# Moving the first head norm group between the gaps of the RWKV chunk steps, and HGRN output products with whole value operands

## The chip, the cores and the metric

The kernel runs as one program on one core of a Trainium2 chip. The metric is the time of the device for the whole program, in microseconds (us), the median over runs. TensorE (PE in the profile) does the matmuls, VectorE (DVE) and ScalarE (ACT) the elementwise work and the sums along a row, GpSimd (POOL) a few gathers, SyncE (SP) issues nearly all transfers. The engines run their own instruction lists in order and wait for each other by semaphores.

## The reference, cut to what matters

The program is one streaming step of a two-layer trunk over 256 prompt frames and 64 sample frames (320 in all), model width 1024.

```
layer 0: x = LN(a*x + [RWKV-7 heads | GLA heads] @ w_out);  x = LN(a*x + SwiGLU(x))
layer 1: x = LN(a*x + HGRN2(x) @ w_out);                    x = LN(a*x + top-2-of-8 experts(x))

RWKV-7, a head of 64:  S_t = S_{t-1} (diag(w_t) - kk_t^T (a_t * kk_t)) + v_t^T k_t ;  o_t = S_t r_t
  then per head and frame:  o = (o - mean(o)) * rsqrt(var(o) + eps) * gn_w + gn_b     (the head norm)
GLA / HGRN2:           S_t = diag(exp(log_a_t)) S_{t-1} + k_t^T v_t ;  o_t = q_t S_t
  GLA: 4 heads, keys 64, values 128.   HGRN2: 8 heads, keys 128, values 128.
```

Both recurrences are worked out in chunks of 64 frames: five chunks, numbers 0 to 3 of the prompt and number 4 of the sample. A chunk's output has two parts, one from the state carried into it and one from inside it. All of it is in 32-bit floats; the dense layers split each operand into a high and a low part of the shorter format `fp32r` and take three products.

## The kernel before

Each engine has one hand-written list of instructions. The dense weights come through a ring of four tiles; ScalarE makes the high half (L2441, `wd_hi`), VectorE the low half (L1468, `wd_lo`), and TensorE takes the three products (L596 to L598, or L609 to L613 where the inputs are only just ready). The experts' weights go the same way at the end (L2916, L2184, L1371 to L1397).

**RWKV chunk steps.** `STEPS = [[0, 4], [1], [2], [3]]`: four steps, the first with two chunks. For each step:
- TensorE multiplies the carried state into the step's first product (L712, `turned_pairs`) and VectorE copies it out (L1765, `w1_done`);
- TensorE takes the next product, ScalarE copies it (L2659, `u_done`), TensorE finishes the state's update (L696, `each(dh, ...)`) and then the step's output, which ScalarE copies to `Osb` (L2666, `o_done`);
- VectorE adds and scales the state `H` (L1784, L1785, `h_done`), for which the next step waits.

The head norm works on `Osb` in two groups: places 0 to 2 (the first two steps, 768 columns, `NEARLY = 3`) and places 3 and 4 (512 columns). For each group VectorE sums (L1738, `norm_totals`), scales the sum and subtracts it (L1746, L1747, `norm_centred`), ScalarE squares (L2645), VectorE sums the squares (L1752, `norm_squares`), ScalarE takes Ln and Exp (L2651, L2652, `norm_std`) and VectorE scales (L1758, `norm_scaled`, `gn_done`). TensorE then turns the rows back (`rows_back`, L991): the first group's after `gn_done` 1, the second's after `gn_done` 2. Around them it does the gla updates (L696 again, in a bank that `h_done` 4 frees) and the gla outputs (L805); VectorE makes the four gla states (L1805) in between the instructions of the second group's norm. ScalarE copies the gla outputs (L2588) and rounds the first input of the next dense layer (L2597), and VectorE makes its low part (L1817).

**HGRN.** The projections of the HGRN layer are taken two output blocks of 128 columns at a time, in two halves of the inputs, and between these halves and behind them stand pieces of the attention: rows turned (L1150, L1155), scores of a level (L1133), state updates (L1179, `hgrn_updates`), the carried part of an output (`hgrn_carried(c)`, L1167, once for each of the chunks 1 to 4), and at the end the parts from inside the chunks (`hgrn_inside(h)`, L1201, for the two halves of the heads). VectorE renews the state of a chunk (L2070) after the carried product of the same chunk has read the old one (`hgrn_o_full`). ScalarE copies the carried products out, VectorE adds the inside parts to them (L2087).

The TensorE array of 128 by 128 can be used in parts. In `hgrn_carried` the weights are 128 rows (keys) by 64 columns (half of the values), and the two halves go to the two halves of the output's rows. In `hgrn_inside` the weights are 64 rows (frames) by 64 columns; chunks of even number lie in the lower rows, those of odd number in the upper ones, so four quadrants are used in turn.

Of the kernel before, what the change touches and what calls it, by code (L numbers as in the profile page):

```python
# [19 lines left out]
C = 64  # L20
NCH = T // C
N_PROMPT_CH = T_PROMPT // C
# [19 lines left out]
HH, HD = 8, 128  # L42
# [33 lines left out]
def mixed_trunk(nc, ins, outs):  # L76
    ctx = ExitStack()
    with ctx:
# [206 lines left out]
        he = tok(h_.take(HH * T), HH)  # L285
# [10 lines left out]
        def place_of(c, hh):  # L296

            par, m_ = (c % 2, 4 * (c // 2) + hh) if c < N_PROMPT_CH else (hh // 2, 8 + hh % 2)
            return slice(64 * par, 64 * par + 64), m_
# [148 lines left out]
        def S(name):  # L448
            name = shared.get(name, (name, 0))[0]
            if name not in names:  # L450
                names[name] = sem(name)
            return names[name]

        def at_count(name, value=1):

            return S(name), shared.get(name, (name, 0))[1] + value
# [52 lines left out]
        def chunk(c):  # L509
            return slice(c * C, (c + 1) * C)  # L510
# [42 lines left out]
        def _(pe):  # L553
# [605 lines left out]
            def hgrn_carried(c):  # L1159

                pe.wait_ge(*(at_count("hgrn_s", c) if c < N_PROMPT_CH else at_count("hgrn_state_in", 16)))
                pe.wait_ge(*at_count("hgrn_qk", len(OPERANDS)))
                b = take(("hgrn_carried", c), "hgrn_o", c)
                for f in range(HH):
                    for half in range(2):
                        values = slice(64 * half, 64 * half + 64)
                        mm = pe.matmul(b[values, f * C:(f + 1) * C], hs[:, 0 if c < N_PROMPT_CH else 1, f, values], he[:, f, chunk(c)],  # L1167
                                       start=f == 0, stop=f == HH - 1, skip_group_check=True)
                mm.then_inc(S("hgrn_o_full"), 1)

            def hgrn_updates(first, second):
# [15 lines left out]
            def hgrn_inside(h):  # L1187

                pe.wait_ge(*at_count("hgrn_sc", 2 * (2 * LEVELS + h) + 2))
                for last in range(2):  # L1190
                    two = [take(("hgrn_inside", h, 2 * last + par), "hgrn_sum", 4 * h + 2 * last + par + 1) for par in range(2)]
                    which = [[(2 * par + i, N_PROMPT_CH) for i in range(2)] if last else
                             [(hh, par + 2 * j) for hh in range(4) for j in range(2)] for par in range(2)]
                    n = len(which[0])
                    for i in range(n):
                        for turn_ in range(2):
                            for par in range(2):
                                rows, m_ = place_of(which[par][i][1], which[par][i][0])
                                half = turn_ ^ par
                                values = slice(64 * half, 64 * half + 64)  # L1200
                                mm = pe.matmul(two[par][values, i * C:(i + 1) * C], hv_rows[rows, h, m_, values],  # L1201
                                               h_sc[rows, h, m_, :], start=i == 0, stop=i == n - 1, skip_group_check=True)
                                if turn_ and i == n - 1:
                                    mm.then_inc(S("hgrn_o_full"), 1)

            def hgrn_sums(h):

# [247 lines left out]
        def _(dve):  # L1455
# [199 lines left out]
            def chain_operands(a):  # L1655
                n_, F = a["name"], a["F"]
                dve.wait_ge(*at_count(n_ + "_e", LEVELS + 2))
                dve.tensor_tensor(a["KD"], a["KD"], a["k"], ALU.mult).then_inc(S(n_ + "_qk"), 1)
                dve.wait_ge(*at_count(n_ + "_e", LEVELS + 1))
                dve.tensor_tensor(a["Z"], a["E"], a["q"], ALU.mult)  # L1660
                dve.tensor_copy(ends[:, 0:F, :], a["E"].rearrange("p f (c t) -> p f c t", c=NCH)[:, :, :, C - 1])\
                   .then_inc(S(n_ + "_qk"), 1)
# [98 lines left out]
            for i, step in enumerate(STEPS):  # L1761
                n = len(step)
                place = PLACE[step[0]]
                dve.wait_ge(*at_count("seq_full", 4 * i + 1))
                dve.tensor_copy(by_pair(W1s[:, place:place + n]), of_pair(where["w1", i], n))\  # L1765
                   .then_inc(S("w1_done"), 1)
                if i == 0:
                    gla_select(LEVELS)
                elif i == 1:
                    chain_operands(gla)  # L1770
                elif i == 3:
                    dve.wait_ge(*at_count("gla_qk", 2))
                    dve.wait_ge(*at_count("gla_state_in", 16))
                    norm_centred(0, NEARLY)
                    norm_squares(0, NEARLY, 0)
                dve.wait_ge(*at_count("seq_full", 4 * i + 3))
                for j, c in enumerate(step):
                    h = H[:, 0 if c < N_PROMPT_CH else 1]
                    d = where["dh", i][:, j * CW:(j + 1) * CW].rearrange("p (f n) -> p f n", f=RF)
                    decay = dC[:, :, c:c + 1].to_broadcast([P, RF, RN])  # L1780
                    if c == 0:
                        mul = dve.tensor_tensor(h, d, decay, ALU.mult)
                    else:
                        link(dve.tensor_tensor(h, h, d, ALU.add))  # L1784
                        mul = dve.tensor_tensor(h, h, decay, ALU.mult)  # L1785
                mul.then_inc(S("h_done"), 1)
                dve.wait_ge(*at_count("h_done", i + 1))
                if i == 2:
                    dve.wait_ge(*at_count("o_done", 2))
                    norm_totals(0, NEARLY)  # L1790
            norm_scaled(0, NEARLY, 0)
            dve.wait_ge(*at_count("o_done", len(STEPS)))
            norm_totals(NEARLY, NCH)
# [625 lines left out]
        def _(act):  # L2419
# [235 lines left out]
            for i, step in enumerate(STEPS):  # L2655
                n = len(step)
                place = PLACE[step[0]]
                act.wait_ge(*at_count("seq_full", 4 * i + 2))
                act.activation(by_pair(U[:, place:place + n]), of_pair(where["u", i], n), ACT.Copy)\  # L2659
                   .then_inc(S("u_done"), 1)  # L2660
                if i == len(STEPS) - 1:
                    norm_squares(0, NEARLY, 0)
                    gla_rows(3, 5)
                    norm_std(0, NEARLY, 0)
                act.wait_ge(*at_count("seq_full", 4 * i + 4))
                act.activation(by_pair(Osb[:, place:place + n]), of_pair(where["o", i], n), ACT.Copy)\  # L2666
                   .then_inc(S("o_done"), 1)
            act.wait_ge(*at_count("gla_ds_full", 1))
            act.activation(gla_s[:, 0].rearrange("p f n -> p (f n)"), where["gla_ds", 0][:, 0:2 * GDV], ACT.Copy).then_inc(S("gla_s"), 1)
            half_rounded(2 * OUT_T + 1)  # L2670
# [593 lines left out]
```

## Time and profile before

| | |
|---|---|
| median of 3 runs | 1468.73 us (1468.45 to 1468.87) |
| profiled execution: its time | 1469.37 us |
| its span, first to last instruction | 1467.7 us |
| TensorE matmuls busy | 1428.1 us (97%) |
| weight loads busy | 1278.1 us (87%) |
| VectorE busy | 1173.1 us (80%) |
| ScalarE busy | 950.7 us (65%) |
| mean granted clock | 0.995 |

The profile is of one execution. Busy times of TensorE overlap: a matmul's record lasts from its start until its last result, and the next one starts earlier than that. So the distance between the starts of two records, the pitch, says more of a small matmul's cost than its length. What counts for the program is the chain that ended last: at each point the work that the next work had to wait for.

### The profile page before, as it was taken

The page shows a single profiled execution, that of the slowest core. Times are in us where ns is not written, and L with a number is a line of the kernel's source. Part 1 is how long each engine was busy: PE and PEld are TensorE (multiplying, and loading weights), DVE is VectorE, ACT ScalarE, POOL GpSimd, SP SyncE. Part 2 cuts the span into 40 slices and gives each one's busy share as a digit, 9 for nine tenths or more (in the row PEclk, how much of TensorE's full clock was granted, in tenths as well). Part 3 has the DMA queues.
Part 4 walks back from the last instruction along what each step waited for, and adds up shares of the span by engine and source line. Part 5 has one row for each costly group of instructions (what it writes and reads, how often), then busy time and mean ns, then how long its engine had stood idle before and what let it go on. Part 6 is the DMA issues. An engine that isn't in the chain of part 4 may idle for free.

```text
span 1467.7 us, 29198 instructions
## 1 busy us (share of the span) xinstructions
PE 1428.1 (97%) x11253; PEld 1278.1 (87%) x11254; DVE 1173.1 (80%) x1580; ACT 950.7 (65%) x1257; POOL 76.3 (5%) x152
## 2 busy tenths in 40 slices
PE   7999989999999999999999999999999999999997
PEld 7999988999999899888788888888888888888884
DVE  5686579545535789867998998899988999898997
ACT  4465455433323696476778787778777887877873
POOL 8300000000000000000000000000000000000000
PEclk9999999999999999999999999999999999999999
DMA  8431004544445262217999999999999999999992
GB/s 261 152 106 37 2 15 145 173 144 145 150 143 164 88 187 88 88 59 285 339 390 397 402 394 398 347 396 380 371 397 350 407 379 362 397 353 410 390 345 93
DMA packets 162214, 371.62 MB, mean 253 GB/s; under 512 B 10232, under 2 KB 85968, under 8 KB 162128
## 3 DMA queue, kind: packets, MB, share of 16 engines
q1 hardware_dynamic: 159352, 361.18, 67.2%
q0 software_dynamic: 2160, 7.87, 2.0%
q8 instruction: 61, 1.00, 0.3%
q10 hardware_dynamic: 616, 1.37, 0.2%
q14 instruction: 25, 0.20, 0.0%
HBM read 360.68 MB, written 9.71 MB: 252 GB/s over the span
## 4 chain that ended last, share of the span: by engine, by line
PE 88%; DVE 7%; ACT 3%; issue 1%; DMA 1%; SPq 0%; DVEq 0%; ACTq 0%
PE psum L1371 11%; PE psum L1372 11%; PE psum L1373 11%; PE psum L596 10%; PE psum L598 9%; PE psum L597 9%; PE psum L1395 5%; PE psum L1397 5%; PE psum L1396 5%; PE psum L712 2%; PE psum L1380 1%; PE psum L696 1%; PE psum L1133 1%; DVE wd_lo L1468 1%; PE psum L609 1%
## 5 line engine op out<-in xcount | busy, mean ns | idle before, releaser
L2184 DVE TENSOR_TENSOR w_lo<-moe_ring,w_hi 128x1024 fp32r<-128x1024 f32 (+1 forms) x560 | 608.3, 1155 | 28.9 <-ACT w_hi L2916 28.9
L2916 ACT ACTIVATE w_hi<-moe_ring 128x1024 fp32r<-128x1024 f32 (+1 forms) x560 | 531.6, 1015 | 69.4 <-PE psum L1397 39.0
L1371 PE MATMUL psum<-w_hi,xe_hi 128*128 128x512 f32 (+1 forms) x768 | 288.1, 375 | 1.6 <-DVE w_lo L2184 1.4
L1372 PE MATMUL psum<-w_hi,xe_lo 128*128 128x512 f32 (+1 forms) x768 | 285.9, 372 | 0.0
L1373 PE MATMUL psum<-w_lo,xe_hi 128*128 128x512 f32 (+1 forms) x768 | 285.4, 372 | 0.0
L1468 DVE TENSOR_TENSOR wd_lo<-arena,wd_hi 128x1024 fp32r<-128x1024 f32 x141 | 169.9, 1208 | 132.9 <-ACT wd_hi L2441 132.6
L596 PE MATMUL psum<-in_hi,wd_hi 128*128 128x320 f32 x800 | 250.5, 313 | 2.5 <-DVE wd_lo L1468 1.2
L2441 ACT ACTIVATE wd_hi<-arena 128x1024 fp32r<-128x1024 f32 (+1 forms) x140 | 146.2, 1047 | 157.4 <-PE psum L598 151.8
L598 PE MATMUL psum<-in_hi,wd_lo 128*128 128x320 f32 x800 | 247.2, 309 | 0.0
L597 PE MATMUL psum<-in_lo,wd_hi 128*128 128x320 f32 x800 | 247.1, 309 | 0.0
L1371 PEld LDWEIGHTS psum<-w_hi,xe_hi 128*128 128x128 f32 x768 | 144.5, 188 | 28.4 <-DVE w_lo L2184 2.9
L1373 PEld LDWEIGHTS psum<-w_lo,xe_hi 128*128 128x128 f32 x768 | 144.2, 188 | 25.8
L1372 PEld LDWEIGHTS psum<-w_hi,xe_lo 128*128 128x128 f32 x768 | 144.5, 188 | 24.9
L596 PEld LDWEIGHTS psum<-in_hi,wd_hi 128*128 128x128 f32 x800 | 150.1, 188 | 5.7 <-issue 1.8
L597 PEld LDWEIGHTS psum<-in_lo,wd_hi 128*128 128x128 f32 x800 | 150.2, 188 | 0.4
L598 PEld LDWEIGHTS psum<-in_hi,wd_lo 128*128 128x128 f32 x800 | 150.2, 188 | 0.0
L1395 PE MATMUL psum<-w_hi,gt_hi 128*128 128x512 f32 x256 | 101.3, 396 | 0.2 <-DVE w_lo L2184 0.2
L1397 PE MATMUL psum<-w_lo,gt_hi 128*128 128x512 f32 x256 | 99.7, 389 | 0.0
L1396 PE MATMUL psum<-w_hi,gt_lo 128*128 128x512 f32 x256 | 99.7, 389 | 0.0
L596 PE MATMUL psum<-hid_hi,wd_hi 128*128 128x320 f32 x224 | 69.7, 311 | 1.3 <-DVE wd_lo L1468 1.3
L598 PE MATMUL psum<-hid_hi,wd_lo 128*128 128x320 f32 x224 | 69.1, 309 | 0.0
L597 PE MATMUL psum<-hid_lo,wd_hi 128*128 128x320 f32 x224 | 69.1, 309 | 0.0
(449 smaller groups left out, 1799.5 us busy)
## 6 DMA issues: line engine op xcount, KB each, us to landing
moe_ring<-in_moe_w SPq DMA_DIRECT2D x216, 1024.0 KB, 8.8
moe_ring<-in_moe_w SPq DMA_DIRECT2D x64, 768.0 KB, 5.7
arena<-in_ffn_w SPq DMA_DIRECT2D x30, 1024.0 KB, 5.3
arena<-in_w_in_c SPq DMA_DIRECT2D x16, 1024.0 KB, 5.5
arena<-in_w_in_ab SPq DMA_DIRECT2D x12, 1024.0 KB, 5.5
arena<-in_w_out_ab SPq DMA_DIRECT2D x4, 1024.0 KB, 5.1
arena<-in_w_out_c SPq DMA_DIRECT2D x4, 1024.0 KB, 5.0
arena<-in_ffn_w SPq DMA_DIRECT2D x4, 768.0 KB, 4.3
```

The lines of the kernel that those rows point to most:

```text
L596: pe.matmul(b[:, 0:T], w_[0][:, cols], x_hi, start=start, stop=False)
L597: pe.matmul(b[:, 0:T], w_[0][:, cols], x_lo, start=False, stop=False)
L598: return pe.matmul(b[:, 0:T], w_[1][:, cols], x_hi, start=False, stop=stop)
L1371: pe.matmul(b[:, 0:w], xe_hi[:, k, :], hi_[:, c0:c1], start=(k == 0), stop=False)
L1372: pe.matmul(b[:, 0:w], xe_lo[:, k, :], hi_[:, c0:c1], start=False, stop=False)
L1373: mm = pe.matmul(b[:, 0:w], xe_hi[:, k, :], lo_[:, c0:c1], start=False, stop=(k == KC - 1))
L1395: pe.matmul(E_Y[half][:, :], g_hi[:, g], hi_[:, cols], start=first, stop=False)
L1396: pe.matmul(E_Y[half][:, :], g_lo[:, g], hi_[:, cols], start=False, stop=False)
L1397: mm = pe.matmul(E_Y[half][:, :], g_hi[:, g], lo_[:, cols], start=False, stop=final)
L1468: dve.tensor_tensor(wd_lo[:, m_ % DENSE_UNITS, 0:words], src, rounded_of(m_)[:, 0:words], ALU.subtract).then_inc(S("dense_lo"), 1)
L2184: dve.tensor_tensor(w_lo[:, i % UNITS, 0:unit_words(i)], moe_unit(i), w_hi[:, i % UNITS, 0:unit_words(i)], ALU.subtract)\
L2916: act.activation(w_hi[:, i % UNITS, 0:unit_words(i)], moe_unit(i), ACT.Copy).then_inc(S("e_hi"), 1)
```

## The change

It has three parts.

1. VectorE's list in the chunk steps. The first group's sum (`norm_totals(0, NEARLY)`) moves from behind the third step's update to ahead of it, behind that step's copy. In the fourth step the centring stays ahead of the update, but the sum of squares (`norm_squares`) and two waits for gla data move behind it, to the end of the steps.
2. ScalarE's list. `norm_std` of the first group moves from ahead of the last output copy to behind it.
3. TensorE's list. In `hgrn_carried` and `hgrn_inside` the two matmuls on halves of the values become one on all 128 values, with weights of 128 by 128 and 64 by 128.

```diff
--- before.py
+++ after.py
@@ hgrn_carried
                 for f in range(HH):
-                    for half in range(2):
-                        values = slice(64 * half, 64 * half + 64)
-                        mm = pe.matmul(b[values, f * C:(f + 1) * C], hs[:, 0 if c < N_PROMPT_CH else 1, f, values], he[:, f, chunk(c)],
-                                       start=f == 0, stop=f == HH - 1, skip_group_check=True)
+                    mm = pe.matmul(b[:, f * C:(f + 1) * C], hs[:, 0 if c < N_PROMPT_CH else 1, f, :], he[:, f, chunk(c)],
+                                   start=f == 0, stop=f == HH - 1, skip_group_check=True)
                 mm.then_inc(S("hgrn_o_full"), 1)
@@ hgrn_inside
                     for i in range(n):
-                        for turn_ in range(2):
-                            for par in range(2):
-                                rows, m_ = place_of(which[par][i][1], which[par][i][0])
-                                half = turn_ ^ par
-                                values = slice(64 * half, 64 * half + 64)
-                                mm = pe.matmul(two[par][values, i * C:(i + 1) * C], hv_rows[rows, h, m_, values],
-                                               h_sc[rows, h, m_, :], start=i == 0, stop=i == n - 1, skip_group_check=True)
-                                if turn_ and i == n - 1:
-                                    mm.then_inc(S("hgrn_o_full"), 1)
+                        for par in range(2):
+                            rows, m_ = place_of(which[par][i][1], which[par][i][0])
+                            mm = pe.matmul(two[par][:, i * C:(i + 1) * C], hv_rows[rows, h, m_, :], h_sc[rows, h, m_, :],
+                                           start=i == 0, stop=i == n - 1, skip_group_check=True)
+                            if i == n - 1:
+                                mm.then_inc(S("hgrn_o_full"), 1)
@@ VectorE, chunk steps
                 elif i == 1:
                     chain_operands(gla)
+                elif i == 2:
+                    dve.wait_ge(*at_count("o_done", 2))
+                    norm_totals(0, NEARLY)
                 elif i == 3:
-                    dve.wait_ge(*at_count("gla_qk", 2))
-                    dve.wait_ge(*at_count("gla_state_in", 16))
                     norm_centred(0, NEARLY)
-                    norm_squares(0, NEARLY, 0)
                 dve.wait_ge(*at_count("seq_full", 4 * i + 3))
...
                 dve.wait_ge(*at_count("h_done", i + 1))
-                if i == 2:
-                    dve.wait_ge(*at_count("o_done", 2))
-                    norm_totals(0, NEARLY)
+            norm_squares(0, NEARLY, 0)
+            dve.wait_ge(*at_count("gla_qk", 2))
+            dve.wait_ge(*at_count("gla_state_in", 16))
             norm_scaled(0, NEARLY, 0)
@@ ScalarE, chunk steps
                 if i == len(STEPS) - 1:
                     norm_squares(0, NEARLY, 0)
                     gla_rows(3, 5)
-                    norm_std(0, NEARLY, 0)
                 act.wait_ge(*at_count("seq_full", 4 * i + 4))
                 act.activation(by_pair(Osb[:, place:place + n]), of_pair(where["o", i], n), ACT.Copy)\
                    .then_inc(S("o_done"), 1)
+            norm_std(0, NEARLY, 0)
```

## Rows read from the trace of the kernel before

**Rows 1.** The page: granted clock in 40 slices, and the chain by engine.

```profile
PEclk9999999999999999999999999999999999999999
...
PE 88%; DVE 7%; ACT 3%; issue 1%; DMA 1%; SPq 0%; DVEq 0%; ACTq 0%
```

**Rows 2.** VectorE's timeline: start, length, instruction, idle time before it and its releaser.

```profile
187.44 0.42 DVE L1765 COPY arena<-psum 128x256 f32<-128x256 f32 x1 [0.65 <-PE psum L712]
189.73 0.42 DVE L1784 TENSOR_TENSOR arena<-arena,psum 128x256 f32<-128x256 f32 x1 [1.87 <-PE psum L696]
...
190.65 0.95 DVE L1738 TENSOR_REDUCE stat<-arena 128x12 f32<-128x768 f32 x1
191.52 0.41 DVE L1765 COPY arena<-psum 128x256 f32<-128x256 f32 x1
...
193.91 0.95 DVE L1752 TENSOR_REDUCE stat<-arena 128x12 f32<-128x768 f32 x1 [0.91 <-ACT arena L2645]
...
195.68 0.96 DVE L1758 TENSOR_TENSOR arena<-arena,stat 128x768 f32<-128x768 f32 x1
...
198.09 0.60 DVE L1805 SCALAR_TENSOR_TENSOR arena<-arena,ends,psum 128x128 f32<-128x128 f32 x2
...
200.16 0.69 DVE L1758 TENSOR_TENSOR arena<-arena,stat 128x512 f32<-128x512 f32 x1
...
204.44 0.49 DVE L1817 TENSOR_TENSOR in_lo<-arena,in_hi 128x320 fp32r<-128x320 f32 x1 [0.39 <-ACT in_hi L2597]
```

**Rows 3.** ScalarE's timeline, the Ln and Exp of the first group.

```profile
194.90 0.30 ACT L2651 ACTIVATE stat<-stat,eps_gn 128x12 f32<-128x12 f32 x1 [0.25 <-DVE stat L1752]
195.24 0.21 ACT L2652 ACTIVATE stat<-stat 128x12 f32<-128x12 f32 x1
```

**Rows 4.** TensorE's timeline, 186 to 202 us (lengths include the overlap of records).

```profile
186.84 0.93 PE L712 MATMUL psum<-arena 64*64 64x64 f32 x48 [0.75 <-DVE arena L1785]
...
189.00 0.62 PE L696 MATMUL psum<-arena 64*64 64x64 f32 x14
...
190.67 0.93 PE L712 MATMUL psum<-arena 64*64 64x64 f32 x48 [0.75 <-DVE arena L1785]
...
193.90 0.57 PE L696 MATMUL psum<-arena 64*64 64x64 f32 x14
...
195.80 2.29 PE L696 MATMUL psum<-arena 64*64 64x128 f32 x38 [1.03 <-DVE arena L1785]
...
198.82 2.45 PE L805 MATMUL psum<-arena 64*128 64x64 f32 x40
201.20 0.69 PE L991 MATMUL psum<-ident,arena 64*64 64x64 f32 x32
```

**Rows 5.** Groups of matmuls by shape: count, busy us together, mean ns of one.

```profile
L1167 PE MATMUL psum<-arena 128*64 128x64 f32 x128 | 4.6, 225 | 0.0
L805 PE MATMUL psum<-arena 64*128 64x64 f32 x72 | 4.5, 275 | 0.0
...
L1201 PE MATMUL psum<-arena 64*64 64x64 f32 x160 | 2.8, 220 | 0.2 <-DVE arena L2070 0.2
...
L1327 PE MATMUL psum<-rt,ones 128*128 128x8 f32 x6 | 0.8, 256 | 0.0
```

**Rows 6.** TensorE's timeline, 607 to 636 us.

```profile
607.70 1.15 PE L1167 MATMUL psum<-arena 128*64 128x64 f32 x32
...
616.39 2.06 PE L1179 MATMUL psum<-arena 64*128 64x128 f32 x32 [1.37 <-ACT arena L2547]
...
630.54 1.16 PE L1179 MATMUL psum<-arena 64*128 64x128 f32 x16
631.63 2.33 PE L1201 MATMUL psum<-arena 64*64 64x64 f32 x144
...
635.29 0.38 PE L596 MATMUL psum<-in_hi,wd_hi 128*128 128x320 f32 x1 [0.69 <-DVE arena L2087]
```

**Rows 7.** VectorE's timeline, the first state update behind a carried product.

```profile
608.96 2.16 DVE L2070 SCALAR_TENSOR_TENSOR arena<-arena,ends,psum 128x128 f32<-128x128 f32 x8
```

## Prediction

> **What bounds the kernel now.** I read the page's chain first. TensorE (PE) holds 88% of it, and its clock row shows full speed, the 2.4 GHz level, in every slice [rows 1]. So an edit counts if it lengthens TensorE's own work or makes TensorE start a stage later. Two stretches are touched: the RWKV chunk steps and what follows them (186 to 204 us), and the HGRN attention (600 to 636 us). In the first the three compute engines hand work round and each gap is under 2 us, so I read their timelines side by side [rows 2 to 4]. In the second TensorE is nearly always busy, so I read the pitch at which small matmuls follow each other, by shape [rows 5], and then the places where TensorE waits or could come to wait [rows 6, 7].
>
> **Part one: the first head norm group.** The steps are numbered 1 to 4 here.
>
> *What it removes.* The 0.95 us sum over 768 columns (L1738) stands behind step 3's update and holds back step 4's copy L1765, which starts at 191.52 as the sum ends. In step 3 that copy followed TensorE's L712 by 0.60 us (186.84 to 187.44). In step 4 TensorE started at 190.67, so the copy could have started at 191.27 [rows 2, 4]: 0.25 us are to be had. The sum moves into VectorE's (DVE's) idle 1.87 us ahead of 189.73, begins about 187.9 and ends about 188.8: free, with 0.9 us of the gap left. If that cover were gone it would cost up to its 0.95. It now waits for step 2's output copy, which ScalarE (ACT) does before its copy for step 3, so before that gap ends.
>
> *Step 4's update.* In step 3 the update (189.73) followed TensorE's L696 (189.00) by 0.73. In step 4 L696 started at 193.90, so the update could have started at 194.63, but the second sum L1752 (193.91, 0.95 us) was ahead of it until 194.86 [rows 2, 4]. With the copy 0.25 earlier the update starts at about 194.4, some 0.45 earlier. TensorE's gla updates (L696 at 195.80, after an idle 1.03 that names this update) start 0.45 earlier too and, 2.02 us long up to their last record, are through at 197.4 instead of 197.8.
>
> *What is late next.* The second sum is now behind the update: 195.2 to 196.15. ScalarE's Ln and Exp (L2651, L2652) were done at 195.45, 0.6 after the sum's end [rows 2, 3]; now at about 196.75. VectorE's next instruction is the scaling L1758, and it waits for them: 196.77 instead of 195.68, **1.09 late**. Everything behind it on VectorE keeps its order and its lengths: the second group's sum, centring, squares and scaling and the four gla states, each 1.09 later.
>
> *Who waits for those.* TensorE's first turn back (L991) needs the first scaling, whose end is now 197.73. TensorE is ready at 197.4 and so starts it where it did: the gain of 0.45 is spent waiting. The gla outputs L805 (198.82) need the first gla state (L1805, done at 198.69, now 199.78) only for their third chunk, after 24 records at 0.056 us, at 200.15: hidden, with 0.37 to spare. The second turn back (L991 at 201.20, no wait in its row) needs the second scaling, which ended at 200.85 and will end at 201.94: TensorE is **0.8 us late** there. The rest of L805, ScalarE's copies of it and the first rounded input follow 0.8 later. VectorE itself is 1.09 late, but it stood idle 0.39 ahead of 204.44, waiting for that rounded input [rows 2], so only 0.7 of it is left and doesn't decide. The chain passes 0.8 on.
>
> Bounds: at best the second turn back isn't late and the 0.45 is kept, -0.45; at worst VectorE's whole 1.09 comes through. I take +0.8, since each step of it has its row.
>
> **Part two: HGRN outputs.** An f32 matmul leaves two records here (64 in four calls of L1167, x128). The pitch is the busy time less one record's length for each stretch, over the other records [rows 5]:
> - L1167, weights 128 rows by 64 columns, two column halves in turn: (4.6 - 4 x 0.225)/124 = 0.030 us. Two run at once, so each takes 0.060.
> - L1201, weights 64 by 64, four quadrants in turn: two stretches, (2.8 - 0.44)/158 = 0.015; each takes 0.060.
> - L805, weights 64 by 128, two row halves in turn, 64 columns moving: two stretches, (4.5 - 0.55)/70 = 0.056; each takes 0.113.
> - L1327, weights 128 by 128, only 8 columns moving: (0.8 - 0.256)/5 = 0.109, alone.
>
> So a record takes 0.06 with 64 weight columns and 0.11 with 128, whatever its rows, and what moves hardly matters: L1179 has L805's weights but 128 moving columns, and its 32 records in 2.06 us give 0.057 [rows 6]. These matmuls are bound by their weights' load.
>
> The change makes L1167's records whole: 16 a call instead of 32, at 0.112 (between L1327's and L805's): 1.79 us against 0.95, **+0.84 a call**. L1201's quadrants take L805's form: 80 records at 0.056, 4.45 us against 2.4.
>
> The Trainium skill ("TensorE: Matmul & The Clock Gate", LDWEIGHTS) gives a weight load as its columns over 1.2 in nanoseconds, rows not counting. By that rule, 107 ns for 128 columns, a call would gain 0.76 us in place of 0.84; the trace's 0.109 agrees with it.
>
> What of it reaches the end [rows 6, 7]:
> - Call 1 (607.70, done at 608.85): VectorE's state update L2070 starts right then, at 608.96, and waits for the call. VectorE and then ScalarE lead on to TensorE's wait ahead of 616.39, so that shifts: +0.84.
> - Call 2 ends in that wait of 1.37 us: its 0.84 is hidden. Without that cover it would cost 0.84.
> - Calls 3 and 4 have no wait around them: +0.84 each.
> - Inside products: before, from 631.63 on, and the dense matmuls behind them started at 635.29 after 0.69 us of waiting for VectorE's sums L2087. Now the last 8 of 80 records start at 631.63 + 72 x 0.056 = 635.65 and the dense matmuls at 636.08; the sums' wait is used up: +0.79.
> - Two switches of the array's division go (dense to call 4, updates to inside). From L1179's 16 records (630.54) to L1201 (631.63) such a switch took about 0.17 over the pitch; together I take -0.25.
>
> Sum: 3 x 0.84 + 0.79 - 0.25 = **+3.1 us**. Bounds: with no wait used up, 4 x 0.84 + 2.1 = +5.4; and if a whole record pitched at 0.056, like the nearest smaller load, about 0 for the calls and +0.6 in all.
>
> **The sum.** 3.1 + 0.8 = +3.9 us. On the profiled execution: span 1467.7 + 3.9 = 1471.6, with the 1.67 around it 1473.3. Its 1469.37 lies 0.64 above the median 1468.73, so the median to expect is 1472.6.
>
> **Rivals.**
> 1. *A small matmul costs by its count, not by its weights.* A whole record would then cost what a half one does, 0.030: 0.48 a call instead of 0.95, -1.4 for the three that show; inside, 80 x 0.030 is 2.4 as before. With part one: 1468.7 - 1.4 + 0.8 = 1468.1, not slower. It decides from a whole record's pitch below 0.07 on. For it speaks that the records halve; against it L1327 and L805. 12%. The Trainium skill ("TensorEngine Tiling (Array Packing)", Instruction Overhead) states such a cost, some 60 cycles a matmul however few its columns; the rows show something larger than that setting the pitch.
> 2. *Part one keeps its gain*: the second turn back isn't late after all. 3.1 - 0.45 = +2.65, 1471.4. For it: spare time of 0.35 at 201.20 and 0.37 at 200.15, and gaps seen in one execution. Against it: 1.09 is more than both. 13%.
> 3. *A whole load can't run under the matmul ahead of it.* The 64 columns then add up to 0.05 a record: 0.16, and 2.6 us a call. Three calls +1.7 each, and the wait before 616.39 no longer covers call 2 (+0.1): 5.2, with 0.79, -0.25 and part one 6.5, so 1475.2. Against it that L805 and L1179 pitch alike. 8%.
> 4. The forecast, +3.9: 67%.
>
> **Numbers.** The forecast's own spread is 3.0 to 4.8 (1471.7 to 1473.5). A measurement of this kernel tells about 0.2%, 2.9 us, from no change, and the forecast is only 1 us beyond that. Faster by more needs -2.9, for which no row offers a source: 0.04. Within: most of rival 1, half of rival 2 and 0.10 of the forecast: 0.26. Slower: the rest, 0.70. The range 1470.4 to 1474.6 leaves out rivals 1 and 3.
>
> **What would show it.** In the chunk steps: the long L1738 ahead of the third update, the last state 0.45 earlier, L1758 about 1.1 later, a wait of some 0.8 us for it ahead of the second L991. In HGRN: calls of 16 records with some 1.9 to 2.1 us busy instead of 1.15, inside products of some 4.7 instead of 2.8, no wait for L2087 behind them. It is wrong if a whole record with 64 columns pitches well below 0.11, or if no wait stands ahead of the second turn back.

## The result and the profile after

The changed kernel took 1476.44 us (median of 5, 1472.72 to 1477.17) against 1468.73 (5 runs beside it, 1468.25 to 1469.39): a ratio of 1.0052, 95% interval 1.0041 to 1.0063. It is slower by 7.7 us where 3.9 were forecast, and outside the range. The profiled execution has a span of 1474.7 us.

The page of the changed kernel, its granted clock in 40 slices and the chain by engine, beside [rows 1]:

```profile
PEclk9999989999999999999999999999999999999998
...
PE 89%; DVE 6%; ACT 3%; issue 1%; DMA 0%; SPq 0%; DVEq 0%; ACTq 0%
```

TensorE still holds the chain. Two slices are new: the sixth (184 to 221 us) and the last show an 8. In the kernel before every slice shows a 9. A 9 stands for 90% or more, not for full speed as the prediction read it. The kernel before has a fall of its own: for 3.4 us, from 687.2 on, its granted clock is at the 1.2 GHz level, behind idle times of 0.86 and 0.44 us among small matmuls. A window on it (busy us and count of PE, PEld, DVE, ACT and POOL, then PEclk, DMA share, GB/s):

```profile
686.00:692.00 6.00, 5.89 (x38) 5.92 (x39) 4.92 (x14) 4.96 (x9) 0.00 (x0) 0.72 1.02 409
```

VectorE's timeline of the changed kernel in the chunk steps, beside [rows 2] (start, length, instruction, idle time and releaser):

```profile
185.44 0.94 DVE L1733 TENSOR_REDUCE stat<-arena 128x12 f32<-128x768 f32 x1
187.39 0.42 DVE L1779 TENSOR_TENSOR arena<-arena,psum 128x256 f32<-128x256 f32 x1 [1.01 <-PE psum L696]
...
188.92 0.42 DVE L1760 COPY arena<-psum 128x256 f32<-128x256 f32 x1 [0.65 <-PE psum L712]
...
192.07 0.42 DVE L1779 TENSOR_TENSOR arena<-arena,psum 128x256 f32<-128x256 f32 x1 [1.65 <-PE psum L696]
...
192.99 0.95 DVE L1747 TENSOR_REDUCE stat<-arena 128x12 f32<-128x768 f32 x1
194.65 0.96 DVE L1753 TENSOR_TENSOR arena<-arena,stat 128x768 f32<-128x768 f32 x1 [0.71 <-ACT stat L2647]
...
197.06 0.60 DVE L1800 SCALAR_TENSOR_TENSOR arena<-arena,ends,psum 128x128 f32<-128x128 f32 x2
```

This execution came to the chunk steps 2.07 us earlier than that of before (each execution arrives within 3 us of another, whatever the kernel), so 2.07 is added to compare. The first sum (185.44) lies in VectorE's gap and leaves 1.01 of it. The last update is at 192.07 + 2.07 = 194.14 instead of the 194.78 in the trace of before: 0.64 early, where about 0.45 was forecast. The scaling L1753 (L1758 before) is at 196.72, 1.04 late; 1.09 was forecast.

TensorE's timeline of the changed kernel in the same place, beside [rows 4]:

```profile
193.10 2.40 PE L696 MATMUL psum<-arena 64*64 64x128 f32 x40 [0.83 <-DVE arena L1780]
195.66 0.93 PE L991 MATMUL psum<-ident,arena 64*64 64x64 f32 x48 [0.17 <-DVE arena L1753]
197.75 3.06 PE L805 MATMUL psum<-arena 64*128 64x64 f32 x40 [1.16 <-issue]
200.74 1.13 PE L991 MATMUL psum<-ident,arena 64*64 64x64 f32 x32
201.80 3.68 PE L805 MATMUL psum<-arena 64*128 64x64 f32 x32
```

The first turn back starts where it did (197.73 with the offset; 197.82 before). But the wait isn't ahead of the second turn back, where 0.8 us was forecast: 200.74 shows none. It is 1.16 us ahead of the gla outputs, and ends 0.09 after VectorE's first gla state (197.06 + 0.60). Soon behind it everything is stretched: 40 records of L805 take 3.06 us instead of 2.45, 32 of L991 1.13 instead of 0.69, 32 of L805 3.68 instead of 2.00.

Windows on the changed kernel, behind the wait (columns as above):

```profile
195.00:215.00 20.00, 18.67 (x208) 17.33 (x204) 16.09 (x32) 10.29 (x22) 0.00 (x0) 0.74 0.00 1
197.75:199.40 1.65, 1.65 (x30) 1.65 (x31) 1.47 (x4) 0.87 (x4) 0.00 (x0) 1.00 0.00 0
199.40:209.60 10.20, 10.20 (x95) 9.85 (x93) 7.66 (x18) 4.87 (x10) 0.00 (x0) 0.50 0.01 2
200.00:210.00 10.00, 10.00 (x90) 9.65 (x89) 7.46 (x17) 4.27 (x10) 0.00 (x0) 0.52 0.01 2
```

The first of these windows on the kernel before:

```profile
195.00:215.00 20.00, 18.11 (x254) 16.49 (x256) 18.27 (x37) 13.01 (x29) 0.00 (x0) 1.00 0.01 2
```

The granted clock was still full for 1.65 us behind that wait, fell to the 1.2 GHz level at 199.4 and stayed there for 10.2 us. This is the term that the prediction doesn't have.

TensorE's timeline of the changed kernel in HGRN, beside [rows 6]:

```profile
609.51 1.89 PE L1165 MATMUL psum<-arena 128*128 128x64 f32 x16
...
618.93 2.06 PE L1177 MATMUL psum<-arena 64*128 64x128 f32 x32 [0.72 <-ACT arena L2542]
...
635.53 4.58 PE L1196 MATMUL psum<-arena 64*128 64x64 f32 x80
640.04 0.42 PE L596 MATMUL psum<-in_hi,wd_hi 128*128 128x320 f32 x1
```

And its groups by shape, beside [rows 5] (count, then busy us and mean ns of one):

```profile
L1165 PE MATMUL psum<-arena 128*128 128x64 f32 x64 | 7.6, 271 | 0.0
...
L1196 PE MATMUL psum<-arena 64*128 64x64 f32 x80 | 4.6, 271 | 0.0
```

By the prediction's own reading, a whole record pitches at (7.6 - 4 x 0.271)/60 = 0.109 us (0.112 taken) and L1196's at (4.6 - 0.271)/79 = 0.055 (0.056 taken). Half of the wait of 1.37 us ahead of the second call's follower is used up (0.72 left), and the wait for the sums behind the inside products is gone. All as forecast.

The program's end, TensorE's timeline of the changed kernel:

```profile
1455.28 3.57 PE L1443 MATMUL psum<-arena,pick_r 128*128 128x512 f32 x4 [2.00 <-ACT arena L2944]
```

and of the kernel before:

```profile
1449.34 1.98 PE L1448 MATMUL psum<-arena,pick_r 128*128 128x512 f32 x4 [0.85 <-ACT arena L2949]
```

Neither edit touches these instructions, yet the first comes 1.15 us later behind the work ahead of it, and the four take 3.57 us, since the granted clock of 1455 to 1459 us is 0.57.

To place the difference I cut each trace at five TensorE or VectorE rows that every kernel has. Chunk steps: from VectorE's first instruction of step 1's update (181.58 in the kernel before) to TensorE's first matmul with ones behind the gla outputs (209.06). HGRN: from the first carried call (607.70) to the first matmul with ones behind the inside products (638.88). End: from TensorE's first down product behind the last turn of the experts (1428.5) to the end of the span. What lies ahead of the first cut is the start. In us:

```
kernel               chunk steps   between    HGRN   between    end    span
before                  27.48      398.64    31.18   789.62    39.2   1467.7
after                   31.42      398.58    34.15   789.64    41.4   1474.7
after, run again        28.25      398.57    34.14   789.59    40.3   1471.9
norm only               31.25      398.69    31.17   790.93    39.1   1471.2
HGRN only               27.05      398.54    34.15   789.62    40.7   1468.8
HGRN only, again        27.18      398.54    34.15   789.63    40.9   1470.5
after, both fillings    28.27      398.58    34.14   789.62    39.1   1469.0
```

Chunk steps +3.94, HGRN +2.97, end +2.2, start -2.07: together +7.0, which is 1474.7 - 1467.7. The second stretch between is 1.4 us longer in four traces (790.9 to 791.1: norm only, its first filling, its two fillings, and its state moved first). All four have a fall of the granted clock there for 3.4 us, at 694 to 701 us, among the first products of the experts. In the kernel before and in the changed one that fall comes earlier, within 48 smaller records (L1431, 7.22 us instead of 5.60), and a wait for VectorE behind them takes it up: three traces with no fall at either place (second filling, wait added, half width) have the stretch no shorter than the kernel before. Why it comes at one place or the other, or not at all, isn't explained. The changed kernel's own account doesn't need it, but the times of "norm only" may hold some of it.

### The profile page after: what moved, and what is told of

Its sections match the earlier page's. It is cut to its first block, busy times and chain, and to the rows that moved or that the text cites. A ratio compares the mean times of both kernels' runs of the same rounds, so it can differ in the third digit from the quotient of the medians.

```text
span 1474.7 us, 28910 instructions
## 1 busy us (share of the span) xinstructions
PE 1437.1 (97%) x11109; PEld 1287.2 (87%) x11110; DVE 1173.0 (80%) x1580; ACT 950.4 (64%) x1257; POOL 76.0 (5%) x152
## 3 DMA queue, kind: packets, MB, share of 16 engines
q10 hardware_dynamic: 616, 1.37, 0.2%
## 4 chain that ended last, share of the span: by engine, by line
PE 89%; DVE 6%; ACT 3%; issue 1%; DMA 0%; SPq 0%; DVEq 0%; ACTq 0%
PE psum L1366 11%; PE psum L1367 11%; PE psum L1368 11%; PE psum L596 9%; PE psum L597 9%; PE psum L598 9%; PE psum L1390 5%; PE psum L1392 5%; PE psum L1391 5%; PE psum L712 2%; PE psum L1375 1%; PE psum L1133 1%; DVE wd_lo L1463 1%; PE psum L696 1%; PE psum L609 1%
## 5 line engine op out<-in xcount | busy, mean ns | idle before, releaser
L2911 ACT ACTIVATE w_hi<-moe_ring 128x1024 fp32r<-128x1024 f32 (+1 forms) x560 | 531.5, 1014 | 70.5 <-PE psum L1392 39.1
```

The costliest lines, as they stand in the source:

```text
L2911: act.activation(w_hi[:, i % UNITS, 0:unit_words(i)], moe_unit(i), ACT.Copy).then_inc(S("e_hi"), 1)
```

## The experiments

Times are medians of n executions, beside the kernel before on the same chips: 1468.23 (18) for the first four kernels, 1468.43 (25) for the next four, 1468.49 (29) for four more, 1468.54 (21) for the last three. "Mean clock" is TensorE's over an execution. In these 93 executions of the kernel before it was never under 0.994. I call an execution fallen by its mean clock when it shows 0.993 or less. That is a sign and no proof: the profiled execution of the kernel with the wait added has the long fall and a mean of 0.995.

**Each part alone, the idle filled, and the sum's move alone** (first four).

Part one alone (the lines of the diff in VectorE's and ScalarE's chunk steps):

```diff
+                elif i == 2:
+                    dve.wait_ge(*at_count("o_done", 2))
+                    norm_totals(0, NEARLY)
...
+            norm_squares(0, NEARLY, 0)
```

> The change's head norm part alone; HGRN as before. Theory A (the second part of the loss is TensorE's clock): the wait ahead of the gla outputs L805 (1.16 us in the trace after) and the 10 us at half clock from about 200 us on both come from this part, so in most runs it is 3.7 to 4.7 us slower than before (1 us of wait, 3 us of half clock), and a run whose granted clock stays near 0.995 to 0.998 is only about 1 us slower. Rival B (the HGRN part costs more than its 3.0 us somewhere): this part costs 1 us or less in all runs.

Measured: 1472.96 us (1472.5 to 1474.46, n 5), ratio 1.0036 [1.0022, 1.0049]; mean clock 0.991 to 0.993 in every run. TensorE's timeline of this kernel:

```profile
196.00 0.93 PE L991 MATMUL psum<-ident,arena 64*64 64x64 f32 x48 [0.17 <-DVE arena L1758]
198.09 3.71 PE L805 MATMUL psum<-arena 64*128 64x64 f32 x40 [1.16 <-issue]
201.73 1.13 PE L991 MATMUL psum<-ident,arena 64*64 64x64 f32 x32
```

The same wait and the same stretch behind it; chunk steps 31.25 us. Part one has this loss by itself, so it isn't an effect of both parts together.

Part two alone:

```diff
-                    for half in range(2):
-                        values = slice(64 * half, 64 * half + 64)
-                        mm = pe.matmul(b[values, f * C:(f + 1) * C], ...)
+                    mm = pe.matmul(b[:, f * C:(f + 1) * C], ...)
```

> The HGRN part alone, chunk steps as before. Theory A: +3.0 us (2.8 to 3.3), as its stage shows in the trace after, about 1471.7, with the granted clock of the kernel before. Rival B: +6 to +8 us. Rival C (whole operands cost by the count of matmuls): 0 or less.

Measured: 1472.51 (1470.53 to 1473.86, n 6), 1.0031 [1.0019, 1.0044]: +4.3, outside the 2.8 to 3.3 that were expected. The HGRN stretch is 34.15, as in the changed kernel; the chunk steps are untouched. The end is 40.7 instead of 39.2: it is this part that brings the late end with it.

The changed kernel with TensorE kept busy by transposes that nobody reads:

```diff
+            pe.wait_ge(*at_count("gla_sc", LEVELS + 2))
+            keep_turning(bank[score_at], 6)
...
-            go = [take(("gla_o", par, 0), "gla_o", par + 1) for par in range(2)]
+            go = [take(("gla_o", 0, 0), "gla_o", 1)]
+            keep_turning(go[0], 10)
+            go.append(take(("gla_o", 1, 0), "gla_o", 2))
```

> The changed kernel with 6 transposes of 128x128 into an idle bank ahead of the gla updates and 10 ahead of the gla outputs, both where TensorE waits. They compute nothing that is used. Theory A (the clock falls because TensorE is idle twice in 5 us): no half clock from 200 us on, and the time falls by about 3 us to 1473. Rival D (the clock falls for another reason, e.g. because of the chip or of what ran before): no change, 1476.4, or worse by the filler's own length.

Measured: 1472.03 (1470.81 to 1473.46, n 7), 1.0026 [1.0015, 1.0038]; mean clock 0.995 to 0.999. Chunk steps 28.27: more work on TensorE, and 3.15 us less. The end is back at 39.1. What is left is +3.8 us; the trace has 0.8 and 2.96 of it in the two stretches, as forecast.

The first sum's move alone:

```diff
+                elif i == 2:
+                    dve.wait_ge(*at_count("o_done", 2))
+                    norm_totals(0, NEARLY)
```

(and the same lines behind the update removed)

> The kernel before with only the first group's sum moved into the third step's gap. The squares' sum and the Ln and Exp stay ahead of the last state. Theory: the fourth step's copy starts 0.25 us earlier and everything behind it follows, -0.25 us, 1468.5, too little to tell by time, but to be seen in the trace: the last state ends 0.25 earlier and no wait stands ahead of the gla outputs. Rival: the shorter way makes VectorE's L1752 wait on ScalarE and nothing is gained.

Measured: 1468.66 (1466.12 to 1470.54, n 11), 1.0003 [0.9994, 1.0012]. In the trace, step 4's copy follows step 3's update by 1.53 us instead of 1.79: the 0.25 is there, and no timing can tell it.

**Which wait, and what a record costs** (next four).

Whole HGRN records, but only the first 32 of 64 columns moved, in the carried products and in the inside ones alike; the other half of these outputs is left out:

```diff
-                    mm = pe.matmul(b[:, f * C:(f + 1) * C], hs[...], he[:, f, chunk(c)], ...)
+                    mm = pe.matmul(b[:, f * C:f * C + C // 2], hs[...], he[:, f, c * C:c * C + C // 2], ...)
```

> HGRN part alone, but each whole-operand matmul moves only the first 32 of its 64 columns; the other half of those outputs is left out. Theory (the pitch is set by the weights' load): a carried call stays at 1.8 to 1.9 us busy for 16 records (pitch 0.108), inside at 0.054 to 0.056 a record, no time gained. Rival (moving columns count): half the width takes 16 x 0.027 = 0.43 us off a call, 1.45 us.

Measured: 1475.17 (one execution). Its groups by shape:

```profile
L1165 PE MATMUL psum<-arena 128*128 128x32 f32 x64 | 7.5, 271 | 0.0
```

(7.5 - 4 x 0.271)/60 = 0.107: with half the columns a record costs what it did, so the moved columns don't set its pitch. (All four calls lie outside the falls named below.) Rival 1, a cost by count alone, doesn't hang on this kernel: it wanted 0.030 for a record, and 0.109 in the changed kernel had refuted it. The miss is the total. This kernel should have been no slower than "HGRN only", and its HGRN stretch is 38.75 us. A window on it shows why:

```profile
600.00:650.00 50.00, 49.25 (x511) 46.36 (x508) 31.26 (x71) 21.25 (x27) 0.00 (x0) 0.90 0.24 76
```

The same window of before has a PEclk of 1.00. There were two stretches at the 1.2 GHz level: from 616.0 (3.4 us), in state updates that had waited 0.75 us behind a narrower call, and from 636.4 (6.8 us), within the 80 narrower inside products, which follow each other without a wait.

Part one with the first filling only (6 transposes ahead of the gla updates):

> Head norm part alone with 6 unused transposes ahead of the gla updates only (they fill the wait of 0.84 us); the wait of 1.16 us ahead of the gla outputs stays. If idle time anywhere in these 5 us decides the clock: no half clock, 1469.3 (before + 1). If the second, longer wait decides it: half clock from 199 on, 1473.

Measured: 1472.4 (1470.31 to 1474.46, n 8), 1.0028 [1.0017, 1.0038]. Two kinds of runs: in five the mean clock is 0.991 to 0.993 and the median 1473.5, in three 0.994 to 0.997 and 1470.4. The profiled execution is one of the three, with the whole wait:

```profile
196.37 0.93 PE L993 MATMUL psum<-ident,arena 64*64 64x64 f32 x48 [0.17 <-DVE arena L1760]
198.46 1.78 PE L805 MATMUL psum<-arena 64*128 64x64 f32 x28 [1.16 <-issue]
```

Part one with the second filling only (10 transposes ahead of the gla outputs):

> Head norm part alone with 10 unused transposes ahead of the gla outputs only (they fill the wait of 1.16 us); the wait of 0.84 us ahead of the updates stays, as one of 1.03 us does in the kernel before, whose clock doesn't fall. Theory: no half clock, 1469.3. Rival (the first wait or the matmuls' form decides): half clock, 1473.

Measured: 1469.55 (1467.9 to 1471.03, n 10), 1.0008 [0.9999, 1.0017]; mean clock 0.994 to 0.997 throughout, as in the kernel before. TensorE's timeline:

```profile
195.92 0.93 PE L991 MATMUL psum<-ident,arena 64*64 64x64 f32 x48 [0.17 <-DVE arena L1760]
196.78 1.31 PE L586 MATMUL psum<-ident 128*128 128x128 f32 x10
198.02 2.45 PE L805 MATMUL psum<-arena 64*128 64x64 f32 x40
200.40 0.70 PE L991 MATMUL psum<-ident,arena 64*64 64x64 f32 x32
```

L805 starts no earlier behind the first turn back than it did with the wait (2.10 us in this kernel, 2.09 in "norm only"), but runs at 2.45. Filling the one wait of 1.16 us takes the loss from 4.7 us to 1.1. Of these 3.6 us the chunk steps show 3.0 (31.25 to 28.26). Filling the other wait leaves 4.0 of it.

Both fillings on part one:

> Head norm part alone with both fillers: its own cost without the clock. Theory: the one wait that I overlooked, 1.0 us for the first gla state ahead of the gla outputs, is all that is left: before + 1.0 (0.7 to 1.3), no half clock. Rival: the filler's transposes push the outputs back as well, + 1.5 or more.

Measured: 1469.78 (1467.66 to 1471.17, n 11), 1.0008 [0.9999, 1.0017]; mean clock 0.994 to 0.997. The same as the second filling alone.

**Who is waited for; HGRN's two parts; a version to keep** (four more).

Part one, with the first gla state right behind the first scaling and the second right behind the second centring:

```diff
             norm_scaled(0, NEARLY, 0)
+            gla_state(1)
             dve.wait_ge(*at_count("o_done", len(STEPS)))
             norm_totals(NEARLY, NCH)
             norm_centred(NEARLY, NCH)
-            gla_state(1)
+            gla_state(2)
             norm_squares(NEARLY, NCH, 1)
-            gla_state(2)
```

> Head norm part alone, with VectorE making the first gla state directly behind the first scaling and the second one behind the second group's centring. Theory: TensorE's outputs L805 then start right behind the first turn back, without the wait of 1.16 us; the second scaling comes about 0.6 us later still, so the second turn back waits about 1.5 us in its place. The loss moves, it does not go: about +1 to +1.5 us against before if the clock stays, +4 if it falls at the new wait.

Measured: 1471.26 (1468.7 to 1473.06, n 6), 1.0023 [1.0011, 1.0035]. TensorE's timeline:

```profile
195.37 0.93 PE L991 MATMUL psum<-ident,arena 64*64 64x64 f32 x48 [0.17 <-DVE arena L1758]
196.23 2.45 PE L805 MATMUL psum<-arena 64*128 64x64 f32 x40
200.10 0.69 PE L991 MATMUL psum<-ident,arena 64*64 64x64 f32 x32 [1.42 <-DVE arena L1758]
```

The wait ahead of L805 is gone: it was for the first gla state. It comes back, longer, ahead of the second turn back, and in four of the six runs the mean clock is 0.991 to 0.993. The profiled execution isn't one of the four: it has the wait of 1.42 us and no fall behind it. So a wait here goes with the lower clock in most executions, whoever is waited for, but not in all.

HGRN's carried products whole, the inside ones as before:

> Only the carried products with whole values. Theory: + 0.84 for calls 1, 3 and 4, call 2 hidden, less one switch: +2.4 us from the first call to the sums L1212 (31.18 us before).

Measured: 1470.59 (1468.85 to 1472.29, n 10), 1.0017 [1.0007, 1.0026]; HGRN stretch +2.60. TensorE's timeline has one row to mind:

```profile
631.86 2.21 PE L1199 MATMUL psum<-arena 64*64 64x64 f32 x135
635.35 0.62 PE L1199 MATMUL psum<-arena 64*64 64x64 f32 x25 [1.29 <-issue]
```

In the middle of one series of products stands an idle of 1.29 us that nothing in the profile releases. From the update in front of them (630.76) to the first dense matmul behind (635.90) this kernel takes 5.14 us, before takes 4.75 [rows 6], so 0.39 of the 2.60 is that idle's, and 2.2 the calls'.

The inside products whole, the carried ones as before:

> Only the inside products with whole values. Theory: + 0.65 us from the first call to the sums, since VectorE's sums held the dense matmuls behind them for 0.69 us anyway; rival (nothing absorbed): +2.

Measured: 1468.67 (1466.49 to 1469.63, n 10), 1.0000 [0.9991, 1.001]; HGRN stretch +0.79. That is the figure of the prediction's term, but partly by luck: the switch that this edit removes is in the measured 0.79 and wasn't in the term, which is why 0.65 was expected of this kernel. 2.2 + 0.79 = 3.0, and both together measured 2.97.

The sum's move, with the gla updates' banks shifted by one, so that the first of them no longer waits for the last state's bank:

```diff
+            turn[0] += 1
             gla_updates(...)
```

> A version that could beat both: only the first sum moved into the third step's gap, and the gla updates' banks shifted by one, so that they no longer wait for the last state's bank. Theory: updates start about 1 us earlier, outputs L805 still wait for the first gla state, the second turn back starts 0.3 to 0.45 us earlier: -0.3 to -0.45 in all, too little to tell by time. Danger: the wait of TensorE moves ahead of the outputs and the clock may fall there.

Measured: 1468.17 (1466.41 to 1470.34, n 11), 0.9999 [0.999, 1.0008]; chunk steps 27.21. In the trace the wait ahead of the gla updates is gone, and 0.92 us of waiting for the first gla state stand ahead of the gla outputs in its place, with no fall behind them; one of the eleven executions (1470.34) has a mean clock of 0.993. A gain of 0.3 can't be told here. No version beats the kernel before by anything that the timings show.

**The wait alone, and the two again** (last three).

The kernel before with one wait added, for the second gla state, ahead of the gla outputs; nothing is moved:

```diff
+            pe.wait_ge(*at_count("gla_s", 3))
```

> The kernel before, and TensorE waits ahead of the gla outputs L805 for the second gla state instead of the first (1.25 us later); nothing else is moved. Theory: the wait costs 1 us or less at full clock, but the clock now falls to half for about 10 us in most executions, as in the changed kernel: +3 to +4.5 us in those. Rival (the moved norm instructions are needed as well): no half clock, +1.

Measured: 1471.94 (1469.62 to 1474.22, n 11), 1.0021 [1.0012, 1.003]. TensorE's timeline and a window:

```profile
199.14 3.23 PE L805 MATMUL psum<-arena 64*128 64x64 f32 x40 [1.32 <-DVE arena L1806]
202.30 1.13 PE L991 MATMUL psum<-ident,arena 64*64 64x64 f32 x32
```

```profile
195.00:215.00 20.00, 18.68 (x228) 17.59 (x224) 15.47 (x30) 9.47 (x20) 0.00 (x0) 0.74 0.01 2
```

Chunk steps 31.7 us, 10.2 of them from 200.6 on, 1.5 us behind the wait's end, at the 1.2 GHz level. A wait of 1.32 us in the old order does what the change does. It costs 3.4 us, over twice its own length. The mean clock of this profiled execution is 0.995; six of the eleven show 0.993 or less.

The changed kernel again:

> The changed kernel once more, for its spread. Theory: HGRN +3.0 in the trace as before; most executions with half clock near 200 us, at 1475 to 1477; those without near 1472. The half clock ahead of the last matmuls (2.2 us in the first trace) is there in some executions only.

Measured: 1474.67 (1472.62 to 1477.27, n 5), 1.0039 [1.0025, 1.0054]: +6.1, where the first five gave +7.7. The profiled execution, 1473.61 us, has the wait of 1.16 us and no lower clock behind it: chunk steps 28.25. Three of the five have a mean clock of 0.992 or 0.993 and are the slowest (1474.67, 1475.22, 1477.27). With the first measurement, seven of ten executions fell by their mean clock, and it may have been more.

HGRN only, again:

> The HGRN part alone once more, for its spread. Theory: median 3 to 4 above before, with single executions 2 us higher where the clock is at half in the last matmuls. Rival: a steady +4 without such a fall in the trace, then something of HGRN's cost lies outside its stage.

Measured: 1472.24 (1470.46 to 1474.46, n 11), 1.0025 [1.0016, 1.0034]: +3.7. HGRN stretch 34.15, end 40.9: the late end is in both profiled executions of this kernel.

## Why the prediction was right in sign and half in size

**HGRN: right.** Forecast +3.1, measured +2.97. The pitch of a whole record (0.109 against 0.112), the hidden second call, the used-up sums' wait (+0.79 alone) all stand. The Trainium skill's rule for a weight load ("TensorE: Matmul & The Clock Gate", LDWEIGHTS: columns over 1.2 in nanoseconds) gives 107 ns; the 0.109 and, with half the columns moving, 0.107 agree. The two switches were put at -0.25; 3 x 0.84 + 0.79 - 2.97 leaves 0.34. The difference lies at the carried calls, which cost 2.2 alone where 3 x 0.84 were forecast. The second switch saved only 0.09 (1.00 us from the start of the updates to that of the inside products, 1.09 in the kernel before), and the inside products cost about that much more than their term.

**Part one's own cost: right in size, wrong in place.** The failed step is "need the first gla state (L1805, done at 198.69, now 199.78) only for their third chunk, after 24 records at 0.056 us, at 200.15: hidden, with 0.37 to spare", said of the gla outputs L805. It followed the data and not the banks. The outputs take two PSUM banks before their first matmul, and the second was the one that gla_ds had filled. It is free only when the first gla state has read it:

```python
go = [take(("gla_o", par, 0), "gla_o", par + 1) for par in range(2)]
```

[rows 2, 4] had it: L805 started at 198.82, 0.13 behind the end of that state at 198.69. In the changed kernel's two traces it starts 0.09 and 0.10 behind it. The state comes 1.04 late in the first and 0.82 in the second, by the distance from the start of the stretch. Where the clock doesn't fall the stretch takes 28.25 to 28.27 us against 27.48, **+0.8** (up to +1.2 against the 27.05 to 27.48 of the other kernels that leave this stretch alone). It is spent ahead of the gla outputs, and the second turn back is in time. So the forecast's 0.8 is met partly by luck: it was worked out for another wait.

**The clock: the missing term.** The prediction priced every stall at its own length, at one clock. This is the step that cost most. Behind the wait of 1.16 us the granted clock fell for 10.2 us, and the chunk steps took 31.42 instead of 28.3: **+3.1**. Filling that wait takes the loss away and filling the other doesn't; the wait alone, put into the kernel before, brings it. That it is the wait is therefore shown; why the clock falls in at least seven of ten executions and not in the others isn't explained. The one execution of the first five with a mean clock of 0.997 took 1472.72 us, and the changed kernel with both waits filled took 1472.03: with the clock kept, the forecast of 1472.6 holds. For the first of the two that is partly luck, since the late end named below adds up to 2.2 us and the start alone varies by up to 3. The Trainium skill (the same page, Part 1: "the default state is throttled, and activity releases the throttle") could have raised the question, and the traces agree that activity counts: with the wait filled the clock stays up. The kernel before could have raised it too, with its fall at 687 us. The rows [rows 4] show three idle times of 0.75 to 1.03 us among small matmuls with no fall behind them; behind one of 1.16 us, after 48 short turns, there was one.

**The end: the other missing term, +2.2.** TensorE's first last-stage product starts 1.96 us behind the start of ScalarE's L2944, where the kernel before needs 0.81, and the clock is at the lower level there for 3.4 us. All four profiled executions of the changed kernel and of HGRN only show it (40.3 to 41.4 us). No other kernel does (39.1 to 39.2), the ones with a single HGRN edit or with both and the fillings included, so the HGRN work by itself isn't its cause. In the four traces the 16 KB instruction transfers (the page's queue 8) come there in close pairs, 0.3 to 0.4 us apart; in the traces of before, norm only, each HGRN edit alone, both fillings and half width they come singly, over 3 us apart. That would fit instructions that arrive late, as would the idle of 1.29 us without a releaser; it is argued and not shown. It isn't the program's length alone: the half-width kernel has as many instructions (28910) and isn't late. No run separates these, so the cause stays open.

**The sum.** Forecast: 0.8 + 3.1 = 3.9. Shown: 0.8 + 3.1 (clock) + 2.97 + 2.2 (end) = 9.1 in the one profiled execution, which began 2.07 us earlier. Between the medians it is 7.7 and, measured again, 6.1; the executions differ in the start, the end and the fall. Rival 1 is refuted by the pitch of 0.109 where it wanted 0.030. Rival 2 is wrong: 27.48 became 28.25 and not 27.0. Rival 3 is refuted by the same pitch, where it wanted 0.16. None of the three had the clock.

## What to carry to other kernels

Ask of a new stall of TensorE not only how long it is but what clock stands behind it: among short, small matmuls a wait of 1.2 to 1.3 us was followed in most executions by a lower clock, which cost some 3 us more than the wait. A slice row of 9s doesn't rule such falls out; a window with its granted clock does. Look for who owns the destination bank of a stage, not only who makes its operands: a row that starts 0.1 us behind another engine's end may be a dependence that no wait in the rows names. For f32 products with few moving columns (8 to 128 here), what counts is the columns of the weights: splitting a 128-column load over two column halves that run at once is nearly twice as fast as whole records.

## What wasn't expected of the hardware

- The granted clock fell to the 1.2 GHz level for 10.2 us, 1.0 to 1.7 us behind the end of an idle of 1.16 us (changed kernel), 1.16 (norm only) and 1.32 us (wait added), and in the other profiled execution of the changed kernel not at all. With ten useless transposes in that idle (1.31 us busy) it stayed up in the profiled execution, and all ten executions (1467.9 to 1471.03 us) are faster than the five with the idle open (1472.5 to 1474.46).
- Moving 32 instead of 64 columns through the same weights saved nothing (0.107 against 0.109 us) and the clock fell twice where it doesn't with 64 columns: the HGRN stretch took 38.75 us instead of 34.15. This is one execution.
- The kernel before has a fall of 3.4 us too, at 687 us. Where it lies within 48 small records it costs nothing; among the first products of the experts, in four other kernels, it costs 1.4 us.
- A straight series of 160 products with nothing to wait for was broken by an idle of 1.29 us in one kernel, and the last stage began 1.1 to 1.4 us late in two others. Both come and go with edits elsewhere in the program.
